# Front of a one-core decoder kernel: input loads on two DMA queues, first weights split by quarters, the copy into h moved behind

## The reference, cut to what matters

```python
def rmsnorm(x, gain):
    y = x32 * lax.rsqrt(jnp.mean(x32 * x32, axis=-1, keepdims=True) + EPS)
    return y * gain
def swiglu(x, w_gate_up, w_down):
    gate, up = jnp.split(x @ w_gate_up, 2, axis=-1)
    return (jax.nn.silu(gate) * up) @ w_down
h = x                                        # 512 tokens x 1024
for l in range(2):
    h = h + 0.5 * swiglu(rmsnorm(h, ffn1_norm[l]), ffn1_w_gate_up[l], ffn1_w_down[l])
    ...                                      # mixer (gated delta rule, or forgetting attention), memory attention
    h = h + 0.5 * swiglu(rmsnorm(h, ffn2_norm[l]), ffn2_w_gate_up[l], ffn2_w_down[l])
return rmsnorm(h, final_norm)
```

## Time and profile before

| | us |
|---|---|
| median of 3 runs | 1978.05 (1977.42 to 1979.33) |
| the profiled execution, its own time | 1979.04 |
| its span, first to last instruction | 1977.3 |
| PE busy | 1958.8 (99%) |
| DVE, ACT, POOL busy | 901.1, 737.8, 379.0 |
| first matmul of unit 0 | 9.88 |
| first matmul of unit 1 | 24.21 |

### The profile page before, as it was taken

One profiled execution on the slowest core, in us unless ns is written; L12 is line 12 of the kernel. 1 busy time (PEld: TensorE's weight loads), 2 busy tenths in 40 slices (PEclk: granted clock), 3 DMA queues, 4 the chain that ended last, 5 costly groups with the idle time before them and its releaser, 6 DMA issues.

```text
span 1977.3 us, 24705 instructions
## 1 busy us (share of the span) xinstructions
PE 1958.8 (99%) x9747; PEld 1612.9 (82%) x9747; DVE 901.1 (46%) x888; ACT 737.8 (37%) x900; POOL 379.0 (19%) x265
## 2 busy tenths in 40 slices
PE   9999999999999999999999999999999999999998
PEld 7888888888877888888888888888887778888887
DVE  5544334378865543433334443433346554333223
ACT  5422222245544443432222443432235454434212
POOL 1312221113813322111010121211011032121100
PEclk9999999999999999999999999999999999999999
DMA  6243323344221333332334433323351133332321
GB/s 193 86 127 106 106 73 88 105 140 133 84 56 40 86 106 106 85 99 78 97 97 150 127 91 100 97 81 88 102 195 43 43 106 97 95 101 79 117 96 64
DMA packets 313267, 196.16 MB, mean 99 GB/s; under 512 B 18479, under 2 KB 304320, under 8 KB 312690
## 3 DMA queue, kind: packets, MB, share of 16 engines
q1 hardware_dynamic: 310368, 183.08, 31.8%
q10 hardware_dynamic: 1938, 9.00, 1.4%
q0 software_dynamic: 896, 3.16, 0.4%
HBM read 188.75 MB, written 6.46 MB: 99 GB/s over the span
## 4 chain that ended last, share of the span: by engine, by line
PE 92%; POOL 3%; DVE 2%; DMA 1%; ACT 1%; issue 1%; SPq 0%; ACTq 0%; DVEq 0%; POOLq 0%
PE ps L619 29%; PE ps L621 29%; PE ps L620 29%; POOL tri L2560 2%; POOL tri_tmp L2558 1%; DVE w_lo L1800 1%; PE ps L1229 1%; PE ps L1255 0%; PE ps L700 0%; PE ps L690 0%; PE ps L1240 0%; PE ps L970 0%; PE ps L678 0%; PE ps L949 0%; PE ps L1086 0%
## 5 line engine op out<-in xcount | busy, mean ns | idle before, releaser
L619 PE MATMUL ps<-x_hi,w_hi 128*128 128x512 f32 x1792 | 707.6, 395 | 1.4 <-DVE w_lo L1800 1.3
L621 PE MATMUL ps<-x_hi,w_lo 128*128 128x512 f32 x1792 | 698.5, 390 | 0.0
L620 PE MATMUL ps<-x_lo,w_hi 128*128 128x512 f32 x1792 | 698.2, 390 | 0.0
L1321 ACT ACTIVATE w_hi<-raw 128x2048 fp32r<-128x2048 f32 (+1 forms) x182 | 319.7, 1757 | 749.8 <-PE ps L621 749.8
L1800 DVE TENSOR_TENSOR w_lo<-raw,w_hi 128x2048 fp32r<-128x2048 f32 (+1 forms) x182 | 405.2, 2227 | 240.3 <-ACT w_hi L1321 240.3
L619 PEld LDWEIGHTS ps<-x_hi,w_hi 128*128 128x128 f32 x1792 | 336.7, 188 | 75.4 <-issue 4.1
L621 PEld LDWEIGHTS ps<-x_hi,w_lo 128*128 128x128 f32 x1792 | 336.6, 188 | 70.4
L620 PEld LDWEIGHTS ps<-x_lo,w_hi 128*128 128x128 f32 x1792 | 336.9, 188 | 67.9 <-issue 1.0
L1822 DVE TENSOR_TENSOR gate_up<-ps,rstd 128x1024 f32<-128x1024 f32 x88 | 107.8, 1225 | 327.1 <-PE ps L621 326.6
L2515 POOL TENSOR_TENSOR gate_up<-gate_up 128x512 f32<-128x512 f32 x66 | 145.7, 2208 | 565.9 <-ACT gate_up L1448 565.9
L621 PE MATMUL ps<-hid_hi,w_lo 128*128 128x512 f32 x528 | 205.6, 389 | 0.0
(11 more groups left out here) (324 smaller groups left out, 1633.6 us busy)
## 6 DMA issues: line engine op xcount, KB each, us to landing
raw<-in_ffn_w_gate_up SPq DMA_DIRECT2D x174, 512.0 KB, 4.9
raw<-in_ffn_w_down SPq DMA_DIRECT2D x48, 384.0 KB, 3.7
raw<-in_ffn_w_down SPq DMA_DIRECT2D x48, 320.0 KB, 3.0
raw<-in_gdn_w_in SPq DMA_DIRECT2D x26, 512.0 KB, 4.6
raw<-in_ffn_w_down SPq DMA_DIRECT2D x20, 512.0 KB, 4.2
raw<-in_w_out SPq DMA_DIRECT2D x16, 512.0 KB, 4.5
raw<-in_kv_w SPq DMA_DIRECT2D x12, 512.0 KB, 4.5
raw<-in_mem_w_kv SPq DMA_DIRECT2D x8, 512.0 KB, 4.1
```

The costliest lines, as they stand in the source:

```text
L619: nc.tensor.matmul(dst, hi, xh, start=first, stop=False)
L620: nc.tensor.matmul(dst, hi, xl, start=False, stop=False)
L621: return nc.tensor.matmul(dst, lo, xh, start=False, stop=last)
L1321: nc.scalar.activation(w_hi[s][:, 0:n], raw[s][:, 0:n], ACT.Copy).then_inc(hi_ready, 1)
```

## The change

SP and ACT share the front's loads. SP: gains, then the first half of the first weights in two quarters (each 2 x 128 KB, a semaphore for each), then a wait until x's columns 2 and 3 have landed, the second half, a wait until columns 4 and 5 have landed, unit 1. ACT: x column 0 alone, then (behind the table load's activation) column 1 alone and columns 2-3; columns 4-5 behind its first rounded quarter, columns 6-7 behind column 2. The ten small loads go behind columns 4, 5 and 6, and behind the rounding of unit 1. The first weights are rounded and cut in four quarters. PE has 5 filler products before the gains (10 before) and 4 between columns 0 and 1 (6 before, behind both); it transposes columns 2 and 3 behind column 0's matmuls. DVE copies columns into `h` later than their `x_lo`. Two semaphores of a later stage are merged with `tile_done` and `tile_evac`, whose counts rise by 3.

```diff
-FILL_BEFORE, FILL_BETWEEN = 10, 6
+FILL_BEFORE, FILL_BETWEEN = 5, 4
+X_COLS = (0, 1, 2, 4, 6, 8)
...
 @block.sync, "xtr"
-                    load_x(0)
-                    for gu in (0, 1):
-                        sp.dma_start(first_w[:, 0:half, gu, :], ...).then_inc(first_half_in, 16)
-                    load_x(1)
-                    load_x(2)
+                    for c in range(2):
+                        rows = slice(2 * c, 2 * c + 2)
+                        for gu in (0, 1):
+                            sp.dma_start(first_w[:, rows, gu, :], ...).then_inc(first_w_in[c], 16)
+                    sp.wait_ge(x_in[2], 16)
                     for gu in (0, 1):
                         sp.dma_start(first_w[:, half:, gu, :], ...).then_inc(raw_in[0], 16)
-                    load_x(3)
 "up0"
+                        if n == 1:
+                            sp.wait_ge(x_in[3], 16)
...
 @block.tensor, unit()
-                        turn(c + 2)
-                        if c == 0:
-                            pe.wait_ge(first_lo, 1)
-                        if c == KT // 2:
+                        if c == 1:
+                            turn(2)
+                        if c >= 1:
+                            turn(c + 2)
+                        if c in (0, 2, 4):
+                            pe.wait_ge(first_lo, c // 2 + 1)
+                        if c == 6:
                             pe.wait_ge(lo_ready, u0 + 1)
...
                     turn_x(0)
+                    fill(FILL_BETWEEN)
                     turn_x(1)
-                    fill(FILL_BETWEEN)
...
 @block.scalar, "xtr"
-                    (six gains, conv_rows, three of small: ten loads)
+                    load_x(0)
                     act.wait_ge(dve_consts, 2)
                     nc.scalar.activation(small[:, 4:5], ones[:, 0:1], ACT.Square)
+                    load_x(1)
+                    load_x(2)
                     act.wait_ge(tables, 1)
                     for c in range(KT):
                         act.wait_ge(cols_turned, c + 1)
                         feed_hi(...)
                         if c == 0:
-                            act.wait_ge(first_half_in, 32)
-                            nc.scalar.activation(w_hi[0][:, 0:half], ...).then_inc(first_hi, 1)
+                            act.wait_ge(first_w_in[0], 32)
+                            round_quarter(0, first_hi)
+                            load_x(3)
+                        if c == 2:
+                            load_x(4)
+                            act.wait_ge(first_w_in[1], 32)
+                            round_quarter(1, first_hi)
                         if c == 3:
                             act.wait_ge(raw_in[0], weights_landed(0))
-                            nc.scalar.activation(w_hi[0][:, half:], ...).then_inc(hi_ready, 1)
+                            round_quarter(2, first_hi)
+                        if c == 5:
+                            round_quarter(3, hi_ready)
                         if c == 4:
                             act.dma_start(mem_tok[:], mem_rows).then_inc(mem_in, 16)
+                            (one gain load; three behind c == 5; two and conv_rows behind c == 6)
                     round_hi(1)
+                    (three loads of small)
...
 @block.vector, "xtr"
                     for c in range(KT):
                         feed_lo(...)
-                        nc.vector.tensor_copy(h[:, c, :], ...).then_inc(cols_copied, 1)
-                        (halves of w_lo behind c == 0 and c == 3)
+                        c == 0: wait first_hi 1, cut_quarter(0), keep(0)
+                        c == 1: keep(1)
+                        c == 2: wait first_hi 2, cut_quarter(1)
+                        c == 3: wait first_hi 3, cut_quarter(2), keep(2)
+                        c == 4: keep(3)
+                        c == 5: wait hi_ready 1, cut_quarter(3), keep(4)
+                        c >= 6: keep(c - 1)
+                    keep(KT - 1)
                     cut_lo(1)
```

More of the change, by code:

```diff
@@ L367, in build_trunk @@
             "mem_in", "gains_in", "conv_w_in", "small_in"))
-        first_gains_in, first_half_in = sem("first_gains_in"), sem("first_half_in")
-        x_in = [sem(f"x_in{i}") for i in range(KT // 2)]
+        first_gains_in = sem("first_gains_in")
+        first_w_in = [sem(f"first_w_in{c}") for c in range(2)]
+        x_in = [sem(f"x_in{n}") for n in range(X_LOADS)]
         consts = sem("consts")
@@ L1364, in _, with load_x, load_gains, round_quarter @@
                 if kind == "xtr":
[L1366 to L1375 removed]
+                    def load_x(n):
+                        cols = slice(X_COLS[n] * P, X_COLS[n + 1] * P)
+                        act.dma_start(x_tok[:, :, cols], x_rows[:, :, cols]).then_inc(x_in[n], 16)
+                    def load_gains(row, *vecs):
+                        for vec in vecs:
+                            flat = vec if len(vec.shape) == 1 else vec.rearrange("a b -> (a b)")
+                            n = flat.shape[0] // P
+                            act.dma_start(gain_rows[row:row + n, :],
+                                          flat.rearrange("(r c) -> r c", c=P)).then_inc(gains_in, 16)
+                            row += n
+                        return row
+                    load_x(0)
                     act.wait_ge(dve_consts, 2)
                     nc.scalar.activation(small[:, 4:5], ones[:, 0:1], ACT.Square)
+                    load_x(1)
+                    load_x(2)
                     act.wait_ge(tables, 1)
[L1379 removed]
+                    def round_quarter(i, signal):
+                        words = slice(i * FULL_UNIT // 4, (i + 1) * FULL_UNIT // 4)
+                        nc.scalar.activation(w_hi[0][:, words], raw[0][:, words], ACT.Copy).then_inc(signal, 1)
                     for c in range(KT):
@@ L1854, in _, with cut_quarter, keep @@
                     dve.wait_ge(tables, 1)
-                    half = FULL_UNIT // 2
+                    def cut_quarter(i, signal):
+                        words = slice(i * FULL_UNIT // 4, (i + 1) * FULL_UNIT // 4)
+                        nc.vector.tensor_tensor(w_lo[0][:, words], raw[0][:, words],
+                                                w_hi[0][:, words].bitcast(F32), ALU.subtract).then_inc(signal, 1)
+                    def keep(c):
+                        nc.vector.tensor_copy(h[:, c, :], ps[:, 4 + c % 4, :]).then_inc(cols_copied, 1)
                     for c in range(KT):
```

89 lines of the change are left out of this document (48 added, 41 removed).

## The result

Kernels before and after ran in turn, twenty times each. Before took 1977.53 us (1976.75 to 1979.79), after 1981.88 us (1978.26 to 1985.97). The ratio is 1.0021, 95% interval 1.0015 to 1.0027, so the change costs 0.21%, some 4 us. The forecast was 1977.3 with a range up to 1979.6: the sign was wrong, and the time lies outside.

What follows compares the result with a forecast made beforehand. PE, busy 1958.8 of 1977.3 us, was taken to bound the kernel, with unit 1's start as the measure. Of chains ending at 23.3 and 23.5 the later counts, 0.7 us earlier: 1978.05 - 0.7 = 1977.3, range 1975.5 to 1979.6.

Steps and rivals of the forecast that it cites:

- First matmul at 7.3: Unit 0's first matmul on PE starts at 7.3 us against 9.88, 2.6 us earlier; bounds 6.9 to 8.3.
- Columns 2 and 3 at 8.8: x's columns 2 and 3 land at 8.8 us, when PE transposes them after waiting 0.1 us.
- Second half at 13.0, bounds 12.6 to 14.0: Second half of the first weights, held by SP's added wait, lands at 13.0 us.
- DVE's heap, L + 8.1 and L + 10.5: Work piled on DVE behind the second half's landing L: free for unit 1 at L + 8.1, PE starts it at 23.5.
- Column 7 at 16.6: PE transposes x's column 7 at 16.6 us against 18.70, at PE's own pace of 1.83 us a column.
- Unit 1's landing, 17.6 - 0.4 + 0.8 + 1.0 = 19.0, bounds 18.2 to 20.0: Unit 1's second load: 17.6 before, first bytes 0.4 earlier, engines dry 0.8, sharing with memory tokens 1.0 more.
- From ACT's start to PE, 4.3: From ACT starting to round unit 1 to PE starting unit 1 takes 4.3 us, unchanged.
- What it moves, the end moves: Any shift of unit 1's start on PE shifts the end equally, since everything behind is unchanged code; forecast 0.7 us earlier.
- The clock rival: Fewer fillers leave PE's clock low at the first matmuls: unit 1 at 25.6, 1.4 us later, 1979.5; chance 0.14.
- The data rival: Late second half, unit 1 or small loads: unit 1 starts at 24.0 to 25.0, about 1978.3 us; chance 0.15.
- Merged semaphores, small loads, `small` behind the rounding: Side edits each put at nothing; uncovered small loads would make PE wait, an unhidden `small` would show 0.9 us.
- The rule weighed: Loads from different issuing engines interleave on the same 16 DMA engines; a second issuer saves only issuing time, nothing of the 2.6 us.

Runs made afterwards that it cites:

- a1: After, with the memory tokens' load issued behind the rounding of unit 1 instead of behind column 4; 1977.66 us, ratio 0.9997.
- b4: After, with the memory tokens' load behind the rounding of unit 1 and DVE's copies into `h` straight behind each column's low part; 1977.95 us, ratio 1.0000.
- a3: After, with twelve filler products on PE ahead of its wait for unit 1; 1981.37 us, ratio 1.0017.
- d1: After, with the memory tokens' load cut into four loads with 512 B runs instead of 4 KB, at the same place; 1981.79 us, ratio 1.0017.
- e4: After, with only DVE's copies into `h` put straight behind their columns; 1980.60 us, ratio 1.0013.
- z2: Before, with ACT rounding unit 1 three times over and fourteen filler products on PE in the wait for it; 1981.87 us, ratio 1.0022.
- a4: Before, with only the filler products cut to 5 and 4 from 10 and 6; 1979.28 us, ratio 1.0002.
- e1: Before, with x's four loads issued by ACT, ahead of its small loads, instead of SP; 1981.13 us, ratio 1.0013.
- b1: Before, with the memory tokens' load issued behind column 1 instead of column 4; 1977.83 us, ratio 1.0001.
- e3: e2 with the memory tokens' load behind the rounding of unit 1 and the copies into `h` straight behind their columns; 1976.48 us, ratio 0.9995.
- e2: After, with x's loads also on SP's one queue in order of need, without the added waits; 1977.07 us, ratio 0.9994.
- z1: Before, with ACT rounding unit 1 three times over, so that PE waits idle for it; 1984.83 us, ratio 1.0034.
- a2: After, without SP's two added waits, the memory tokens' load staying behind column 4; 1979.57 us, ratio 1.0006.

## Why the prediction was wrong, step by step

- *First matmul at 7.3*: right, 7.33. It varies with the landing: a1, b4, a3, d1 and e4, which start with the same loads, have 7.40, 7.36, 7.98, 8.18 and 8.44. The bounds were 6.9 to 8.3, and so a little narrow.
- *Columns 2 and 3 at 8.8*: right, 8.83. The wait on SP ended at 7.09, when the pair landed, and not at 8.8: PE was the later of the two.
- *Second half at 13.0, bounds 12.6 to 14.0*: 12.21 in after, 0.4 below the bound, 12.33 in b4, 15.05 in a1. The value was fair, the bounds too narrow (e4 13.45, a3 12.85 and d1 12.98 lie inside).
- *DVE's heap, L + 8.1 and L + 10.5*: the mechanism and its size are right where the second half decides (a1: 8.1 and 10.4). In after DVE had been idle for 2.96 us, since the heap wasn't the last chain.
- *Column 7 at 16.6*: 18.11. Column 6 had to wait 1.14 us for x's last pair, issued on ACT's queue at 9.47 and 6.7 us under way. The prediction costed the waits for columns 0 to 3 and gave this pair none, although it named it as sharing the engines. a3 (2.25) and d1 (2.33) show the same wait larger.
- *Unit 1's landing, 17.6 - 0.4 + 0.8 + 1.0 = 19.0, bounds 18.2 to 20.0*: this is the step that failed. It landed at 22.44. The form of the sum was right, one term mis-sized: 1.0 us for the tokens' sharing. The sum without it, 18.0, is what b4 measured without the tokens beside unit 1 (18.4), with engines as thin as in after; with them it is 22.4. So the sharing cost 4 us here where 1.0 was allowed. That the tokens were taken to be issued at about 14 and were at 12.22 doesn't matter, as their bytes ran from 16 us on. The prediction gives no row for its 1.0 us; before's own trace, read by queue over 16 to 18 us, has 0.63 MB of tokens against 0.11 of weights, and would have been the row to start from. Why it came to 4 us and not less the bytes don't explain, and it stays open.
- *From ACT's start to PE, 4.3*: right, 26.73 - 22.44 = 4.29.
- *"What it moves, the end moves"*: right for the start (z2: 4.0 later, 4.15 longer), but incomplete. This is the second step that failed: PE's idle time of 3.5 us brought the low clock, and with it 2.5 us more, a term that the sum didn't have. The clock rival stood in the list for PE's start, from shorter fillers, with 1.4 us; a4 shows no cost there. No rival let a late load bring it. The data rival, unit 1 at 24.0 to 25.0, named the right place with too small a price, and without the clock.
- *Merged semaphores, small loads, `small` behind the rounding*: nothing, right; the gains and the rows of the convolution were no wait in after. Only in a3 were the rows late, by 0.31 us.
- *The rule weighed*: that loads from different issuing engines interleave on the same 16 engines. I had written that what is interleaved comes later, and had let it change nothing in the sum but 1.0 us. With the tokens it came 4 us later. The Trainium skill, "DMA: Bandwidth & Descriptors", section "Queues, rings and completion order", says that an engine takes turns between the queues it has work for, a packet at a time. Our rows agree where both queues have much to move: 440 packets against 435 (e1), 227 against 246 (b1), whatever their length. After's 810 against 339 over 16 to 20 us is no such stretch, since there each queue had work for a part of the time only.

With the two failed terms as they were measured the sum comes out: start 26.73 against 24.21 is +2.5, the low clock +2.5, together 5.0 for the profiled executions. Over the twenty runs of each the medians are 4.35 apart, and after's runs spread from 1978.26 to 1985.97. The mean granted clock listed for the runs points the same way: the three runs at 0.999 took 1978.26, 1979.91 and 1980.38, those at 0.996 and 0.997 took 1980.6 to 1986.0. Only one of these executions was profiled; e4's and d1's profiles, of kernels nearly the same, lose a like time by a late first quarter or by x's last pair. How the 4.35 divides over such causes is not known. What a1 and b4 show is that it goes when the tokens go behind unit 1.

What stays open. Why the same loads, issued at the same times, land up to 1.2 us apart in different executions (5.8 in after, 7.0 in e4), and why the engines were thin in some stretches in which loads were pending, is not settled. Why unit 1's last packets needed until 22.4, when SP's queue moved more than enough bytes before, is open too, and so is how the change as a whole would do with the waits or the quarters alone. The dip at 620 to 640 us, in before and after alike, was not looked into. And whether e3 is a gain (1976.48 against 1977.84, interval from 0.9986 to 1.0005) would take more runs.

## What to carry to other kernels

When loads are moved to a second queue, write down for each load what will be in flight beside it, and take the shares from the trace by queue, in bytes, not from the number of queues: what is needed soon must not share with a large load in long runs that isn't. Write down as well what the issuing engine itself would have done in the time (e1's ACT). Asking for everything on one queue in the order of need gave the same early start within 1.2 us and lost nothing later (e2). And price a wait of PE of some microseconds twice: once for itself, and once for the matmuls at the low clock behind it, 2.5 us in after and 1.4 in z1's profile.

## What the runs showed of the hardware

- Two queues that both have much to move get the engines in turn, packet by packet, and so bytes by their length: 440 packets of 1 KB against 435 of 512 B over 2 us, 0.43 MB against 0.22 (e1); 227 of 4 KB against 246 of 1 KB over 3 us, 0.93 MB against 0.25 (b1). Near the end of a load this no longer holds: 0.82 MB against 0.04 over 18 to 21 us with 512 B on both sides and unit 1 still out (d1).
- Issuing a load takes the issuing engine's time where it has its own work behind it: four issues took ACT 2.28 us in e1, and its table load began at 7.42 and not 4.92.
- The granted clock fell to its low level during or behind idle times of PE of 2.02 us (e4), 2.74 in unit 0 (a2), 3.49 (after), 3.65 (e1) and 4.26 (z1), and stayed at 1.00 behind 1.06 and 2.01 (a1), 2.25 (a3) and 2.33 (d1). So the length of the idle time alone doesn't decide. In after it was back at 1.00 from 33 us on, PE having been busy from 26.73. The Trainium skill, "TensorE: Matmul & The Clock Gate", section "What's actually happening", calls the throttled clock the default that activity lifts; z2, in which fillers keep PE busy and the clock stays up, agrees.
- The clock need not be low when PE starts again: in z1 unit 1's first matmul took 0.50 us, as at the full clock, and the low windows come behind it (0.62 over 28 to 30 us, then 0.52). The loss is to be looked for behind the idle time, not only in it.
